# Products of the undivided linear stages interleaved over their output tiles, two transformer blocks in split fp32 on one core

## The reference

```
# first block, two layers; mod = silu(c) @ w_ada[i] + b_ada[i], cut in six vectors of 1024
h = rmsnorm(x) * (1 + sc1) + sh1
y = mla(h)                                  # layer 0: 8 heads; layer 1: swa(h), 16 heads in windows of 128
x = x + gt1 * y                             # y ends in a product with w_o
h = rmsnorm(x) * (1 + sc2) + sh2
x = x + gt2 * (square(relu(h @ w_ff1[i])) @ w_ff2[i])       # 1024 -> 4096 -> 1024
# second block
h = h + 0.5 * ((silu(n(h) @ w1) * (n(h) @ w3)) @ w2)        # 1024 -> 2816 -> 1024
proj = n(h) @ w_in                          # q, k, v, pooled channels, two gates
y_attn, y_pool = dilated attention, pooling over 2, 4, 8 and 16 tokens
h = h + (g0 * (y_attn @ w_branch_attn) + g1 * (y_pool @ w_branch_pool)) @ w_out
h = h + 0.5 * ((silu(n(h) @ w1) * (n(h) @ w3)) @ w2)
return rmsnorm(h)
```

## Time and profile before

| what | value |
|---|---|
| median of three runs | 2396.2 us (2395.34 to 2396.57) |
| the profiled execution, its own time | 2394.96 us |
| its span from first to last instruction | 2393.1 us |
| PE (matmul) busy | 2283.4 us, 95% of the span |
| VectorE, ScalarE, GpSimd busy | 1227.0, 836.6, 156.4 us |
| matmul records | 11491, of which 7308 have 512 columns and 128 output channels |
| mean granted PE clock | 0.972 of full speed (2.4 GHz; its other level is 1.2 GHz) |

### The profile page before, as it was taken

The page is one execution under the profiler, slowest core; times in us unless marked ns, Lnnn a source line. Parts: engine busy times, 40 slices in busy tenths (PEclk is TensorE's granted clock), DMA queues, the critical chain, the costliest instruction groups (busy, mean ns, idle before and its releaser), DMA issues.

```text
span 2393.1 us, 27739 instructions
## 1 busy us (share of the span) xinstructions
PE 2283.4 (95%) x11491; PEld 1916.0 (80%) x11491; DVE 1227.0 (51%) x1905; ACT 836.6 (35%) x1259; POOL 156.4 (7%) x125
## 2 busy tenths in 40 slices
PE   6897999999988999999989999999999999999999
PEld 3775888888887898888888888887667789888887
DVE  5568667667676664334353433355454545333334
ACT  3555343323255544233233222234342333222222
POOL 7100000000032100000010000011001000000000
PEclk8998999999999999999999999999789999999999
DMA  6213445555421123322313323223101322323220
GB/s 234 88 59 139 141 140 184 186 194 192 166 71 53 36 59 118 101 93 89 105 54 107 105 90 105 76 84 109 36 31 37 131 93 67 123 88 106 88 88 36
DMA packets 143906, 245.43 MB, mean 103 GB/s; under 512 B 4571, under 2 KB 69430, under 8 KB 143654
## 3 DMA queue, kind: packets, MB, share of 16 engines
q1 hardware_dynamic: 142480, 240.60, 30.6%
q0 software_dynamic: 640, 2.70, 0.3%
q10 hardware_dynamic: 662, 0.37, 0.1%
HBM read 241.56 MB, written 2.10 MB: 102 GB/s over the span
## 4 chain that ended last, share of the span: by engine, by line
PE 83%; DVE 8%; ACT 3%; issue 3%; POOL 1%; DMA 1%; SPq 0%; DVEq 0%; ACTq 0%; POOLq 0%
PE PS L66 82%; ACT t L72 3%; DVE t L83 3%; DVE t L75 2%; DVE t L86 1%; PE PS L69 1%; POOL t L79 1%; DMA t<-in_w_ada_dram 1%; DVE t L79 1%; POOL t L75 1%; DVE t L80 0%; DVE PS L75 0%; DVE t L92 0%; DVE t L89 0%; DVE t L95 0%
## 5 line engine op out<-in xcount | busy, mean ns | idle before, releaser
L66 PE MATMUL PS<-t,t 128*128 128x512 f32 (+5 forms) x11124 | 2228.3, 362 | 74.5 <-DVE t L75 22.8
L66 PEld LDWEIGHTS PS<-t,t 128*128 128x128 f32 (+2 forms) x11124 | 1868.1, 190 | 432.0 <-issue 82.3
L72 ACT ACTIVATE t<-t 128x512 fp32r<-128x512 f32 (+8 forms) x569 | 538.7, 963 | 1188.6 <-PE PS L66 660.7
L75 DVE TENSOR_TENSOR t<-t,t 128x2048 fp32r<-128x2048 f32 (+9 forms) x506 | 600.2, 1194 | 680.1 <-ACT t L72 677.6
L72 ACT ACTIVATE t<-PS 128x512 f32<-128x512 f32 (+5 forms) x307 | 162.1, 545 | 201.6 <-PE PS L66 129.4
L75 POOL TENSOR_TENSOR t<-t,t 128x512 f32<-128x512 f32 (+2 forms) x71 | 82.4, 1161 | 1248.8 <-ACT t L72 972.9
L72 ACT ACTIVATE t<-t,t 128x256 fp32r<-128x256 f32 (+5 forms) x212 | 112.3, 536 | 106.2 <-DVE t L83 45.3
L83 DVE SCALAR_TENSOR_TENSOR t<-t,t,t 128x1024 f32<-128x1024 f32 (+2 forms) x149 | 140.3, 946 | 9.9 <-ACT t L72 3.9
L83 DVE SCALAR_TENSOR_TENSOR t<-PS,t,t 128x512 f32<-128x512 f32 (+3 forms) x120 | 76.8, 643 | 97.2 <-PE PS L66 81.8
L75 DVE TENSOR_TENSOR t<-t,PS 128x512 f32<-128x512 f32 (+1 forms) x82 | 53.0, 653 | 103.0 <-PE PS L66 98.9
L69 PE MATMUL PS<-t,t 128*128 128x128 f32 (+1 forms) x367 | 62.5, 318 | 31.4 <-DVE t L79 16.4
(11 more groups left out here) (29 smaller groups left out, 171.5 us busy)
## 6 DMA issues: line engine op xcount, KB each, us to landing
t<-in_w_ff_dram SPq DMA_DIRECT2D x64, 1024.0 KB, 5.3
t<-in_ffn_w_dram SPq DMA_DIRECT2D x60, 1024.0 KB, 5.3
t<-in_w_ada_dram SPq DMA_DIRECT2D x48, 1024.0 KB, 5.4
t<-in_w_in_dram SPq DMA_DIRECT2D x13, 1024.0 KB, 5.1
t<-in_swa_w_qkv_dram SPq DMA_DIRECT2D x6, 1024.0 KB, 5.1
t<-in_ffn_w_dram SPq DMA_DIRECT2D x8, 768.0 KB, 4.3
t<-in_w_in_dram SPq DMA_DIRECT2D x24, 256.0 KB, 3.6
t<-in_mla_w_o_dram SPq DMA_DIRECT2D x4, 1024.0 KB, 6.3
```

What stands on the lines that cost most here:

```text
L66: return Instr(self.real and self.real.matmul(o, lhs, rhs, start=start, stop=stop, **more))
L72: return Instr(self.real and self.real.activation(o, src, func, **more))
L75: return Instr(self.real and self.real.tensor_tensor(o, a, b, op))
```

## The change

`pe_linear` hands its undivided, unswapped calls without hooks to a new function. There the order is unit, then k-tile, then the three kinds of product, and innermost the output tiles: four consecutive products go to four banks, with the same input operand and with four slices of the weight. PE waits for all four banks ahead of the stage's first product. The four tiles are finished by the last four products of the stage. `pe_gate` does the same with two tiles for each weight, in every chunk but the first. Number, sizes and operands of the products stay; the lists of the other engines are the same instruction for instruction.

```diff
+        def pe_interleaved(e, tag, ws, outs, xs, hf, bk, k0s):
+
+            cs = COLS[hf]
+            for n in bk:
+                e.wait_for(banks.free((tag, n, hf)))
+            for u, w in enumerate(ws):
+                pe_step(e, w)
+                for k in range(WT[w]["kt"]):
+                    first, last = u == 0 and k == 0, u == len(ws) - 1 and k == WT[w]["kt"] - 1
+                    xh, xl = xs(e, k0s[u] + k, 0, hf)
+                    for n, (c, wd) in enumerate(outs):
+                        e.matmul(PS[:, bk[n], cs], whi(w)[:, k, c:c + wd], xh, start=first, stop=False)
+                    for n, (c, wd) in enumerate(outs):
+                        e.matmul(PS[:, bk[n], cs], whi(w)[:, k, c:c + wd], xl, start=False, stop=False)
+                    for n, (c, wd) in enumerate(outs):
+                        t = e.matmul(PS[:, bk[n], cs], wlo(w)[:, k, c:c + wd], xh, start=False, stop=last)
+                        keys = [(tag, n, hf)] if last else []
+                        if n == len(outs) - 1 and k == WT[w]["kt"] - 1:
+                            keys.append(("used", w))
+                        if keys:
+                            t.then_inc(acc, *keys)
+            for n in bk:
+                banks.open((tag, n, hf))
+
         def pe_linear(e, tag, ws, outs, xs, until, halves=False, swap=False, mid=None):
...
+                if not halves and not swap and mid is None:
+                    pe_interleaved(e, tag, ws, outs, xs, hf, bk, k0s)
+                    continue
...
+                        if not first:
+                            keys = [(("g", i), c, w, n, hf) for n in range(2)]
+                            for key in keys:
+                                e.wait_for(banks.free(key))
+                            for k in range(8):
+                                xh, xl = xs(e, k, 0, hf)
+                                for n, key in enumerate(keys):
+                                    e.matmul(PS[:, banks[key], :], whi(wt_)[:, k, 128 * n:128 * n + 128], xh,
+                                             start=k == 0, stop=False)
+                                for n, key in enumerate(keys):
+                                    e.matmul(PS[:, banks[key], :], whi(wt_)[:, k, 128 * n:128 * n + 128], xl,
+                                             start=False, stop=False)
+                                for n, key in enumerate(keys):
+                                    t = e.matmul(PS[:, banks[key], :], wlo(wt_)[:, k, 128 * n:128 * n + 128], xh,
+                                                 start=False, stop=k == 7)
+                                    if k == 7:
+                                        t.then_inc(acc, key, *([("used", wt_)] if n else []))
+                            continue
```

More of the change, by code:

```diff
@@ L596, in mm3 @@
             return e.matmul(o, al, bh, start=False, stop=last)
+        def pe_interleaved(e, tag, ws, outs, xs, hf, bk, k0s):
[20 more added lines that the diff above has]
+                banks.open((tag, n, hf))
         def pe_linear(e, tag, ws, outs, xs, until, halves=False, swap=False, mid=None):
-            mid, k0s = mid or {}, []
+            k0s = []
             for w in ws:
@@ L630, in pe_linear @@
                             banks.open((tag, n, hf))
-                        if (hf, u, n) in mid:
+                        if mid and (hf, u, n) in mid:
                             mid[hf, u, n]()
```

## The result

The changed kernel takes 2441.16 us (median of four runs, 2437.4 to 2445.93) against 2395.77 us; the ratio is 1.020, 95% interval 1.0188 to 1.0212. It is slower, by some 45 us. The profiled execution of the change took 2437.4 us, the fastest of its four, and spans 2435.6 us, 42.5 us more than the span of before. So the profiles explain 42.5 of the 45 us.

The account below looks back on a forecast made before the run. PE, busy in 95% of the span, was taken as the bound. Waits and clock, 15.9 + 2.0 + 9.0 + 3.95 + 1.75 + 5.2 = 37.8 us on 2394.96, gave 2432.8, as median 2434 us, range 2418 to 2450.

Parts of the forecast that it names:

- (e): Second q group: eight subtractions end later, delaying the heads' maxima and normalisation queued behind; 3.95 us.
- Clock: Falls of the granted clock at the three modulations behind up stages, 1.7 us each; 5.2 us in all.
- p = 0: Products of 512 columns: one into its predecessor's bank costs nothing extra, so interleaving itself gives 0 us.
- (a): Modulation behind an up stage, three times: later read-outs delay its low parts, PE waits 5.3 us each; 15.9 us.
- (b): Modulation behind a down stage, three times: read-outs end 1.3 us later, covered by VectorE's idle time; 0 us.
- (c): Last modulation, behind (("down", 0, 3), 0): adds and sums of squares end later where PE waits already; 2.0 us.
- (d): Stage starts behind modulation products, six times: predecessor's banks awaited early, three waits of 2.0 and three of 1.0; 9.0 us.
- (f): ("gp", 0): banks of the four pooling products awaited at its start, before the last is read out; 1.75 us.
- upper bound: Clock term's upper end: one fall of 1.7 us for each of nine further waits, 15 us more.
- third rival: The clock falls more often, at each of twelve waits: 2449 to 2456 us, 2454 as its figure; chance 0.08.

Follow-up runs that it names:

- e5: Kernel before, with only the three up stages interleaved whose read-outs are queued ahead of a modulation's low parts, ("up", 0, 1 to 3, 0): 2415.98 us.
- e6: Kernel before, with only the three up stages holding modulation products and the down stages behind them interleaved: 2404.55 us.
- e2: Kernel before, tile after tile, with all banks of an undivided linear stage awaited ahead of its first product: 2396.14 us.
- e9: Changed kernel, with unit 0 tile after tile, each bank awaited at its tile, and only the last unit interleaved: 2427.22 us.
- e11: Kernel before, with only the second q group, ("q", 1), interleaved: 2397.6 us.
- e1: Changed kernel, with the first feed-forward stage's up and down stages, ("q", 1) and ("gp", 0) left tile after tile: 2395.21 us.
- e7: Changed kernel, with the four modulation products issued 24 products later, inside unit 1 of an interleaved stage: 2426.77 us.
- e10: Changed kernel, with tiles interleaved two by two in each unit, each pair's banks awaited ahead of it: 2402.42 us.
- e3: Changed kernel, with the last unit of each undivided linear stage tile after tile and unit 0 still interleaved: 2394.89 us.

## Why the prediction held, point by point

The time forecast was 2434 us with a range of 2418 to 2450; 2441.16 was measured, slower and in the main by the mechanism of the forecast. One term, (e), came out by another cause, and the clock's was too small.

- **Pitch, p = 0.** Held: 226.67 ns with a bank change at every product. The Trainium skill's warm gap (TensorE: Matmul & The Clock Gate, Back-to-back issue gap), 215.8 ns, is not reached by these products in either order.
- **(a), 15.9 us.** The later read-out measured 5.3 us a place. PE's two waits are 4.79 us at the first place and 14.1 us at the three. A wait is counted from the end of a record, which is longer than the pitch: from start to start the two products came 380.44 - 377.07 = 3.4 and 382.49 - 380.67 = 1.8 us late, 5.2 us (377.07 and 380.67 are where the pitch would have put them). e5 has it alone: +13.8 us idle in its stretch. The forecast had the wait end on VectorE's subtraction; 3.21 us of it end on ScalarE's copy of the modulation sum, which comes as late by the same chain.
- **(b), nothing.** Held (e6).
- **(c), 2.0 us.** The wait grew from 1.68 to 3.78 us: 2.1 us.
- **(d), 9.0 us.** Three of 2.1 and three of 1.1 us idle, 9.8 us. e2, e6 and e9 show that it takes the late tiles and the early wait for banks together.
- **(e), 3.95 us of waiting.** This step failed in its mechanism. The wait came (3.31 us) but the waits behind it shrank, and over the window attention the change has 0.5 us more of idle time, e11 0.7 us less. That the stretch still got 3.0 us longer in the change and 3.6 us in e11 is clock; that the term had nearly this amount is luck.
- **(f), 1.75 us.** 1.95 us.
- **Clock, 5.2 us.** Too small: busy time rose by 12.3 us, 7.1 us more than the term. I had costed a fall only at (a), 1.7 us each, taken from the shorter waits of (c). In e5 three places of (a) cost 7.8 us of busy time in the stretch, 2.6 each; e6 adds 2.4 us for the starts and e11 4.2 us for (e). Falls at the rarer waits were in the upper bound and in the third rival, and not in the sum.

At the four places where the waits stayed, (a), (c), (d) and (f), 28.7 us were forecast and 27.9 measured. The page's 30.2 us against 32.6 is partly chance: (e) is missing, and some 2 us of idle time lie elsewhere; e1 has +2.5 us with none of these waits. The forecast had the waits 2.4 us too high and the clock 7.1 us too low; the other 2.9 us between 42.5 and 45.4 us are that the profiled execution is the fastest of its four. That the parts add is shown too: e5 (21.0 us), e6 (9.5 us) and e11 (4.0 us) over their own runs of before make 34.5 us, and (c), the three waits of 1.1 us and (f) have 2.1 + 3.4 + 1.95 = 7.4 us more, 42 of 45 us.

One sum of the range was off: with no fall of the clock and (d) halved, the terms make 15.9 + 2.0 + 4.5 + 3.95 + 1.75 = 28.1 us and not 26, so 2424 and not 2422. It touches the lower bound alone.

What stays open: how much clock a given wait costs. Behind the window attention e7 and e9 have 11.4 and 8.7 us more busy time than before and the change has 0.3, though e7 has the instructions of the change there.

## What to carry to other kernels

Where the profile shows one pitch inside a bank and at bank changes, as for these products of 512 columns, there is nothing to win by turning the banks faster; read that from two stretches with different numbers of products per bank before anything is reordered. What an order of products does decide is when each tile is finished: tiles that end together put all read-outs of a stage behind its end, and this costs only where another engine's list has something queued behind them that PE wants soon. Find these places by following the list behind the read-outs, wait for banks no earlier than their first product, and where interleaving is wanted for another reason, do it in pairs or leave the last unit tile after tile: e10 and e3 cost 9 and 2 us where the full form cost 45.

## What I had not expected of the hardware

- A wait that only moves can still cost: in e11 the idle time was the same, and the time 4.0 us longer (2 to 6 by the interval) at a granted clock of 0.90 against 0.97.
- Longer or bunched waits cost more clock here than in proportion. One wait of 1.48 us at each of three places (e10) left the clock at 1.00 and the busy time at +0.8 us; one of 2.14 us (e6) came with 0.99 and +2.4 us; 3.21 and about 1.4 us in a row (e5) with 0.97 and +7.8 us. These are single executions, and no run tells the length of a wait from the bunching.
